# Output projection as seven block products with sums made under the gated merge, in a one-core encoder block

## The reference, cut to what matters

```
h  = rms_norm(x, norm_mix)                     # x: (1, 512, 1024) float32
q_a, k_a, v_a, q_b, k_b, v_b, u_c, g = split(h @ w_in)
o_a, o_b, o_c = attention_a, attention_b, pooling      # each (512, 512)
merged = sig(g0)*(o_a @ w_branch_a) + sig(g1)*(o_b @ w_branch_b) + sig(g2)*(o_c @ w_branch_c)
x  = x + merged @ w_out                        # (512, 1024) @ (1024, 1024)
h2 = rms_norm(x, norm_ffn)
x  = x + (silu(conv(gate)) * conv(val)) @ w_down,   [gate | val] = h2 @ w_up
```

## Time and profile before

| what | value |
|---|---|
| median of 3 executions | 823.93 us (823.73 to 824.07) |
| the profiled execution | 822.09 us, its span 820.2 us |
| granted TensorE clock, mean | 0.999 |
| TensorE busy | 813.5 us of the span (99%) |
| VectorE, ScalarE, GpSimd busy | 606.3, 407.4, 24.1 us |
| DMA traffic | 113.26 MB, mean 138 GB/s |

### The profile page before, as it was taken

How to read it: one execution, slowest core, us unless ns; L and a number is a source line. 1 busy time by engine, 2 the same in 40 slices (tenths; PEclk the granted TensorE clock), 3 DMA queues, 4 the chain that set the end, 5 groups by cost and what they waited for, 6 DMA issues and landing times.

```text
span 820.2 us, 11715 instructions
## 1 busy us (share of the span) xinstructions
PE 813.5 (99%) x3863; PEld 675.8 (82%) x3863; DVE 606.3 (74%) x893; ACT 407.4 (50%) x572; POOL 24.1 (3%) x42
## 2 busy tenths in 40 slices
PE   8999999999999999999999999999999999999998
PEld 6888888888888888888888888888888888888886
DVE  5958888868668775555554578777777878898797
ACT  6547676656545545434341464334433444565653
POOL 1010000000000060000000000000000000000000
PEclk9999999999999999999999999999999999999999
DMA  6342333222222223333367523665655555576454
GB/s 210 103 130 78 96 85 100 80 63 67 77 77 77 69 73 90 102 91 102 90 219 245 190 78 103 205 193 191 201 190 188 180 185 188 172 221 210 149 182 173
DMA packets 130702, 113.26 MB, mean 138 GB/s; under 512 B 6148, under 2 KB 109544, under 8 KB 129264
## 3 DMA queue, kind: packets, MB, share of 16 engines
q1 hardware_dynamic: 129840, 110.63, 43.0%
q0 software_dynamic: 672, 2.12, 0.9%
q10 hardware_dynamic: 160, 0.14, 0.0%
HBM read 99.21 MB, written 13.65 MB: 138 GB/s over the span
## 4 chain that ended last, share of the span: by engine, by line
PE 98%; DMA 1%; DVE 0%; SPq 0%; issue 0%; DVEq 0%
PE ps L1609 30%; PE ps L1610 30%; PE ps L1611 30%; PE ps L1741 2%; PE ps L1731 2%; PE ps L1756 1%; PE ps L1755 1%; DMA x_in<-in_x_dram 1%; PE ps L1909 0%; DVE out_sb L1594 0%; PE ps L1646 0%; PE ps L1705 0%; PE ps L1724 0%; PE ps L1706 0%; SPq L315 0%
## 5 line engine op out<-in xcount | busy, mean ns | idle before, releaser
L1609 PE MATMUL ps<-h_lo,w_hi 128*128 128x512 f32 x704 | 276.6, 393 | 0.1
L1611 PE MATMUL ps<-h_hi,w_lo 128*128 128x512 f32 x704 | 274.1, 389 | 0.0
L1610 PE MATMUL ps<-h_hi,w_hi 128*128 128x512 f32 x704 | 274.1, 389 | 0.0
L971 DVE TENSOR_TENSOR w_lo<-w_raw,w_hi 128x1024 fp32r<-128x1024 f32 x112 | 138.0, 1232 | 108.0 <-ACT w_hi L535 79.2
L535 ACT ACTIVATE w_hi<-w_raw 128x1024 fp32r<-128x1024 f32 x96 | 101.7, 1060 | 201.7 <-PE ps L1611 201.6
L1611 PEld LDWEIGHTS ps<-h_hi,w_lo 128*128 128x128 f32 x704 | 132.2, 188 | 27.9
L1609 PEld LDWEIGHTS ps<-h_lo,w_hi 128*128 128x128 f32 x704 | 132.2, 188 | 27.4 <-issue 0.3
L1610 PEld LDWEIGHTS ps<-h_hi,w_hi 128*128 128x128 f32 x704 | 132.3, 188 | 26.3
L1456 DVE TENSOR_TENSOR conv_in<-ps,r_ffn 128x512 f32<-128x512 f32 x44 | 30.3, 690 | 23.9 <-PE ps L1611 22.1
L890 ACT ACTIVATE conv_out<-conv_in,par 128x512 f32<-128x512 f32 x44 | 35.5, 806 | 9.7 <-DVE conv_in L1456 9.7
L1444 DVE SCALAR_TENSOR_TENSOR conv_out<-conv_in,par,conv_out 128x512 f32<-128x512 f32 x44 | 33.1, 752 | 5.0 <-DVE conv_out L1441 1.1
(11 more groups left out here) (238 smaller groups left out, 1304.1 us busy)
## 6 DMA issues: line engine op xcount, KB each, us to landing
w_raw<-in_w_in_dram SPq DMA_DIRECT2D x103, 256.0 KB, 3.1
w_raw<-in_w_up_dram SPq DMA_DIRECT2D x88, 256.0 KB, 3.2
raw_t<-in_w_down_dram SPq DMA_DIRECT2D x11, 1024.0 KB, 8.7
down_sums<-t_sum SPq DMA_DIRECT2D x11, 1024.0 KB, 5.7
w_raw<-in_w_down_dram SPq DMA_DIRECT2D x33, 256.0 KB, 3.0
w_raw<-down_sums SPq DMA_DIRECT2D x33, 256.0 KB, 3.9
w_raw<-in_w_out_dram SPq DMA_DIRECT2D x16, 256.0 KB, 3.2
w_raw<-down_sums SPq DMA_DIRECT2D x22, 128.0 KB, 3.0
```

What stands on the lines that cost most here:

```text
L971: v.tensor_tensor(w_lo[:, slot, :], w_raw[:, slot, :], r32(w_hi[:, slot, :]), ALU.subtract)\
L1609: mm3(dst, l_hi, r_lo, start=start, stop=False, **kw)
L1610: mm3(dst, l_hi, r_hi, start=False, stop=False, **kw)
L1611: return mm3(dst, l_lo, r_hi, start=False, stop=stop, **kw)
```

## The change

The output projection is written as a product of 2x2 blocks with seven products: the 1024 channels are four pairs p of two 128-channel blocks, the tokens two halves of 256, the columns two halves of 512.

- For each pair, `factor_sums` makes four sums of token halves of the merged blocks (`mst`), and `factors_hi`/`factors_lo` split seven 256-column factors (`mx_hi...`, `mx_lo...`). For pairs 0, 1 and 2 this stands inside the merge loop, for pair 3 behind it.
- For each pair, four sums of weight quarters are needed. GpSimd's queue loads the raw rows (1 MB), VectorE makes the sums (`set_of_sums`), GpSimd's queue stores them (1 MB). Six such sets (four of `w_out`, two of `w_down`) stand in the merge of blocks m = 1 to 6. The two of `w_down` were made in the output projection before.
- TensorE does pass X (four quarters of each pair, 96 matmuls) and pass Y (three quarters of each pair, 72 matmuls), adding Y onto banks that hold X's products. ScalarE keeps three products (`kept`), VectorE adds them into `x1`, which now holds the input from the start. The transposes behind it run in another order (`H2_ORDER`, `H2_BANK`).
- At the start, token tiles 1 and 2 are issued from ScalarE's queue, one dummy matmul more is done, and the transposes of tile 1 stand behind the first product, those of tiles 2 and 3 behind the second.
- The loops over m on ScalarE and VectorE are written out.

```
+NO = KD // 2
+MX = 7 * HT
+H2_ORDER = (4, 5, 6, 7, 0, 1, 2, 3)
+H2_BANK = (2, 3, 6, 7, 0, 1, 4, 5)
-WARM = (3, 3)
+WARM = (3, 4)
...
 SyncE
-            for t in range(1, TT):
-                x_load(t, 0)
+            x_load(3, 0)
...
+            def out_load(m, halves):
+                s, u = m // 2, m % 2
+                if m < 2:
+                    sp.wait_ge(lo_ready, N_OUT - 1 + u)
+                elif m == 3:
+                    sp.wait_ge(unit_done, N_OUT)
+                elif m > 3:
+                    sp.wait_ge(ow_lo, m - 3)
+                for dst, src in halves:
+                    sp.dma_start(dst, src).then_inc(d_landed[2 * (s % 2) + u], 16)
...
+            out_x(1, 0)
+            out_x(0, 0)
+            out_x(0, 1)
+            out_x(1, 1)
+            for p in (2, 3):
+                for u in range(2):
+                    out_x(p, u)
+            sp.dma_start(x1[:, :, :], xw).then_inc(x1_landed, 16)
+            out_y(0)
             pair_load(2)
+            for p in range(1, NO):
+                out_y(p)
...
 GpSimd
+            pool.wait_ge(pl_ready, 4)
+            for q in range(NO + 2):
...
+                pool.dma_start(wraw_o[:, :, :, :], rows_q).then_inc(set_landed, 16)
+                pool.wait_ge(t_ready, q + 1)
+                pool.dma_start(sums_q, wsum_o[:, :, :].rearrange("p (o j) c -> p o j c", o=1)).then_inc(set_stored, 16)
...
 ScalarE
+            for t in (1, 2):
+                a.dma_start(x_in[:, t, 0:WB], xw[:, t, 0:WB]).then_inc(x_landed[t][0], 16)
...
+            def factors_hi(p):
+                a.wait_ge(mst_ready, p + 1)
+                dst = factors(mx_hi01, mx_hi23, p)
+                act(dst[:, 0:HT], mp[:, 0, 0:HT], ACT.Copy)
+                act(dst[:, HT:5 * HT], mst[:, :], ACT.Copy)
+                act(dst[:, 5 * HT:MX], mp[:, 1, :], ACT.Copy).then_inc(mx_hi_ready, 1)
+
+            for m in range(KD):
+                i, n, last_m = m % 2, N_MERGE + 3 * m, m == KD - 1
+                ...
+                last.then_inc(sig_ab, 1)
+                hi(n + 2, i)
+                if last_m:
+                    out_hi(0)
+                else:
+                    hi(n + 3, 1 - i)
+                a.wait_ge(unit_done, n + 2)
+                if m:
+                    a.wait_ge(mg_ready, m)
+                act(mg[:, 3, :], ps[:, 4 * i + 2, :], ACT.Sigmoid, bias=pcol(BG, m + 2 * KD)).then_inc(sig_c, 1)
+                if last_m:
+                    out_hi(1)
+                else:
+                    hi(n + 4, i)
+                if m >= 2 and i == 0:
+                    factors_hi(m // 2 - 1)
...
+            for m in (2, 3, 4):
+                out_hi(m)
+            factors_hi(NO - 1)
+            for m in range(5, 10):
+                out_hi(m)
+            a.wait_ge(x1_acc, 1)
+            a.wait_ge(mx_lo_ready, NO)
+            kept(o1, 0)
+            a.wait_ge(ow_done, 2 * NO - 1)
+            kept(o5, 2)
+            out_hi(10)
+            a.wait_ge(ow_done, 2 * NO)
+            kept(o7, 6)
+            for m in range(11, 4 * NO):
+                out_hi(m)
...
+            a.wait_ge(ow_done, 4 * NO - 3)
             hi(N_UP, 0)
+            a.wait_ge(ow_done, 4 * NO - 2)
+            hi(N_UP + 1, 1)
             x1_square(0)
+            for j in range(4):
+                h2_split_hi(j)
             x1_square(1)
+            for j in range(4, KD):
+                h2_split_hi(j)
             x1_square(2)
             x1_square(3)
...
 VectorE
+            def set_of_sums(q):
+                d.wait_ge(set_landed, q * 16 + 16)
+                if q:
+                    d.wait_ge(set_stored, q * 16)
+                sums_first(wraw_o, wsum_o)
+                sums_second(q, wraw_o, wsum_o)
+
+            def factor_sums(p):
+                a11, a21, a12, a22 = mp[:, 0, 0:HT], mp[:, 0, HT:S], mp[:, 1, 0:HT], mp[:, 1, HT:S]
+                s2, s1, s3, s4 = (mst[:, q * HT:q * HT + HT] for q in range(4))
+                d.wait_ge(mg_ready, 2 * p + 2)
+                v.tensor_tensor(s1, a21, a22, ALU.add)
+                v.tensor_tensor(s3, a11, a21, ALU.subtract).then_inc(mst_step, 1)
+                ...
+                v.tensor_tensor(s2, s1, a11, ALU.subtract).then_inc(mst_step, 1)
+                ...
+                v.tensor_tensor(s4, a12, s2, ALU.subtract).then_inc(mst_ready, 1)
+
+            def factors_lo(p):
+                d.wait_ge(mx_hi_ready, p + 1)
+                dst, h = factors(mx_lo01, mx_lo23, p), factors(mx_hi01, mx_hi23, p)
+                v.tensor_tensor(dst[:, 0:HT], mp[:, 0, 0:HT], r32(h[:, 0:HT]), ALU.subtract)
+                v.tensor_tensor(dst[:, HT:5 * HT], mst[:, :], r32(h[:, HT:5 * HT]), ALU.subtract)
+                v.tensor_tensor(dst[:, 5 * HT:MX], mp[:, 1, :], r32(h[:, 5 * HT:MX]), ALU.subtract).then_inc(mx_lo_ready, 1)
+
+            for m in range(KD):
+                i, n, bank, last_m = m % 2, N_MERGE + 3 * m, 4 * (m % 2), m == KD - 1
                 lo(n + 2, i)
...
                 v.tensor_tensor(mg[:, 0, :], mg[:, 0, :], mg[:, 1, :], ALU.add).then_inc(mg_step, 1)
+                if last_m:
+                    out_lo(0)
+                else:
+                    lo(n + 3, 1 - i)
+                if m >= 2 and i == 0:
+                    factors_lo(m // 2 - 1)
                 d.wait_ge(sig_c, m + 1)
                 d.wait_ge(unit_done, n + 3)
                 v.tensor_tensor(mg[:, 2, :], ps[:, bank + 3, :], mg[:, 3, :], ALU.mult).then_inc(mg_step, 1)
                 d.wait_ge(mg_step, m * 3 + 3)
+                if m >= 2:
+                    d.wait_ge(mx_lo_ready, m // 2)
+                v.tensor_tensor(mp[:, i, :], mg[:, 0, :], mg[:, 2, :], ALU.add).then_inc(mg_ready, 1)
+                if last_m:
+                    out_lo(1)
+                else:
+                    lo(n + 4, i)
+                if i == 1 and not last_m:
+                    factor_sums(m // 2)
+                if 1 <= m <= NO + 2:
+                    set_of_sums(m - 1)
+
+            out_lo(2)
+            out_lo(3)
+            factor_sums(NO - 1)
+            out_lo(4)
+            factors_lo(NO - 1)
+            for m in range(5, 10):
+                out_lo(m)
...
+            out_lo(15)
             lo(N_UP, 0)
...
             lo(N_UP + 1, 1)
+            d.wait_ge(x1_acc, 3)
+            v.tensor_tensor(rows_of(0, 0), rows_of(0, 0), ps[:, 0:2, :], ALU.add).then_inc(x1_ready, 1)
+            d.wait_ge(ow_done, 4 * NO - 1)
+            d.wait_ge(x1_step, 5)
+            v.tensor_tensor(rows_of(0, 1), rows_of(0, 1), ps[:, 2:4, :], ALU.add).then_inc(x1_ready, 1)
+            for t in (2, 3):
...
+                v.tensor_tensor(x1[:, t, 0:S], x1[:, t, 0:S], ps[:, t + 4, :], ALU.add).then_inc(x1_ready, 1)
...
 TensorE
             x_transposes(0, 0)
             warm(1)
-            x_transposes(1, 0)
...
-                    if t == 0:
-                        x_transposes(kk + 2, 0)
+                    if t == 0 and kk == 0:
+                        x_transposes(1, 0)
+                    elif t == 0:
+                        x_transposes(2, 0)
+                        x_transposes(3, 0)
...
+            for p in range(NO):
+                start, stop, e = p == 0, p == NO - 1, p % 2
+                pe.wait_ge(mx_lo_ready, p + 1)
+                pe.wait_ge(ow_lo, 2 * p + 1)
+                first = out_quarter(p, 0, 0, e, 0, 0, start, stop)
+                ...
+                out_quarter(p, 2, 2, e, 0, 1, start, stop)[1].then_inc(ow_done, 1)
+                pe.wait_ge(ow_lo, 2 * p + 2)
+                if start:
+                    pe.wait_ge(mg_ready, KD)
+                sixth = out_quarter(p, 4, 1, e, 1, 0, start, stop)
+                ...
+                out_quarter(p, 6, 3, e, 1, 1, start, stop)[1].then_inc(ow_done, 1)
```

More of the change, by code:

```diff
@@ L51 @@
 N_OUT = N_MERGE + 3 * KD
-N_UP = N_OUT + KD
+N_UP = N_OUT
 N_DOWN = N_UP + 2 * KF
@@ L1884, in _ @@
                 merge(mm, 1, False)
-            def out_unit(k, slot, first=False, last=False):
-                pe.wait_ge(lo_ready, k + (N_OUT + 1))
-                pe.wait_ge(m_lo_ready, k + 1)
-                for b8 in range(8):
-                    t, h = b8 // 2, b8 % 2
-                    if first and b8 == 4:
-                        pe.wait_ge(mg_ready, KD)
-                    tk, c = slice(t * P, t * P + P), slice(h * S, h * S + S)
-                    done = product(ps[:, b8, :], m_hi[:, k, tk], m_lo[:, k, tk], w_hi[:, slot, c], w_lo[:, slot, c],
-                                   first, last)
-                    if last and (h == 1 or t == TT - 1) and b8 < 7:
-                        done.then_inc(x1_acc, 1)
-                done.then_inc(unit_done, 1)
@@ L1902, in _, with out_quarter @@
-            pe.wait_ge(mg_ready, KD - 1)
-            for k in range(KD):
-                out_unit(k, k % 2, first=k == 0, last=k == KD - 1)
+            def out_quarter(p, bank, at, e, u, h, start, stop, **kw):
```

(7 more changed lines are left out.)

285 lines of the change are left out of this document (166 added, 119 removed).

## The result

Six executions of the changed kernel take 852.66 us by their median (851.66 to 853.16), six of the kernel before 823.75 us (822.67 to 824.07). The ratio is 1.0355, with an interval of 1.0344 to 1.0365: 29 us slower, where I had forecast 3. The profiled execution's span is 851.5 us, 31.3 more than before.

A forecast was written before the change was run, and what follows sets the result against it. TensorE, busy 99% of the span, bounds the kernel. From the profiled 822.09 us: -5.4 matmuls, +7.3 factors, +1.0 output projection and transition, +0.1 start give 825.1, or 826.9 us as median (0.36% slower); range 823.4 to 831.5.

The forecast's parts named there:

- weight sums in the merge: Merge: VectorE's added sums fit and GpSimd's sets land in time; taken as 0, upper bound 4.4 us.
- Factors inside the merge: Merge blocks 2, 4, 6: factor work delays lo(n+4), stalling TensorE 2.45 us each; +7.3 us, bounds 6.6 to 8.1.
- Rival 5: Merge: clock drops to 1.2 GHz for 12 matmuls behind each stall; +8.2 us, 835.1 us in all; chance 0.05.
- Matmuls removed: Output projection: 168 matmuls instead of 192, at 0.227 us each; 5.4 us less.
- Output projection and transition: Output projection through transition to the up projection: thin places in operand supply cost 1.0 us, bounds 0.3 to 2.5.
- low part 4: Transition: this low part of the transposed operand comes after TensorE wants it; 0.65 us, up to 1.6.
- half-pair 10: Transition: its weights may land a microsecond late behind x1's 2 MB and `pair_load`'s 1 MB, raising 0.65 to 1.6 us.
- The stall for half-pair 5: Output projection: out_lo(5), behind the last pair's factor work, is ready at 13.8 but wanted at 13.6; 0.2 us.
- Start: Kernel start: second weight half may land later behind two token tiles; +0.1 us, bounds -0.2 to +1.3.
- Rival 4: Merge: sets come late because GpSimd's round trip takes 14 us; +4.4 on the forecast, 831.3 us; chance 0.10.

The follow-up runs named there:

- e4: Changed kernel with GpSimd's store and next set load held back until SP has issued the gate unit's weights: 836.31 us, ratio 1.0148.
- b2: Kernel before plus GpSimd's traffic alone (1 MB stored and 1 MB loaded in merge blocks 2 to 5, values unused): 829.07 us, ratio 1.0066.
- e2: Changed kernel with the sets' transfers cut to a sliver after the first set, so the right sums are left out: 835.43 us, ratio 1.0137.
- e3: Changed kernel with the factors' copies moved on ScalarE from behind hi(n+4) to behind hi(n+2): 834.98 us, ratio 1.0122.
- e5: Changed kernel with both merge mends, GpSimd's transfers held back and the factors' copies moved earlier: 828.16 us, ratio 1.0065.
- e8: Changed kernel with both merge mends, four output projection mends and the start of the kernel before: 820.96 us, ratio 0.9971.
- b1: Kernel before with the new start alone (token tiles from ScalarE's queue, one more dummy matmul, transposes reordered): 824.65 us, ratio 1.0014.
- e1: Changed kernel with the start of the kernel before: 851.8 us, ratio 1.0331.
- e7: Changed kernel with both merge mends, four output projection mends (x1 in pieces, `pair_load` later, two order changes) and the new start: 822.05 us, ratio 0.999.
- e9: Changed kernel with the four output projection mends alone, the merge as the change left it: 846.81 us, ratio 1.0295.
- e6: e5 with the x1 load in four pieces among the weight loads and the third down pair's load behind the last weights: 828.89 us, ratio 1.0064.

## Why the prediction was wrong

**The step that failed** is the one on the weight sums in the merge, "I take 0". I asked of GpSimd's 2 MB per block only whether the set itself lands in time for VectorE. It does: 7.9 us for the load, 4.8 for the store, and VectorE never stood for a set anywhere in the merge. I did not ask who is issued behind these transfers. Two engines are released by nearly the same moment, GpSimd by the last sum (352.5) and SP by the low part of unit n+2 that follows it (353.7), so the 2 MB stand in front of the one load with the least slack. The upper bound of 4.4 us was worked out from the wrong victim. What the runs showed in place of the 0: the waits in the merge are 19.0 us with the collision and 6.7 without it (e4), and the whole kernel takes 16.3 us less without it.

This step does not carry the whole miss. Without the collision e4 still takes 836.3 us, above my range, through the lower clock in the merge, the output projection and the start, which follow below.

**The two causes use up one slack.** The traffic alone costs 4.4 us of waiting in four blocks (b2), the order of the factors alone 6.7 in three (e4). Together they cost 19.0. In b2's expectation I called this multiplying; the working shows that the delays add in one chain, and the slack is taken off once. The gate unit has 5.4 us from the block's start until TensorE asks, and its own copy and subtraction take 2.4 of them. With the 0.2 at the block's start that leaves 2.8 us. In the border shown, the late load takes 3.2 (362.69 against 359.46) and the factors' work between the copy and its subtraction 5.2 (7.55 less 2.4): 3.2 + 5.2 - 2.8 = 5.6, and TensorE waited 5.33. Either alone would leave 0.4 or 2.4; e4 has 2.2 to 2.3, b2 0.7 to 1.5 (in the border shown its load came later still, 4.7 us into the block against 3.4). Taking away either one (e2, e4 the traffic, e3 the order) gave 16 to 18 us back, taking away both 24 (e5).

**Factors inside the merge: +7.3.** Right in place, sign and size: 2.18, 2.17 and 2.31 us in e4 against 2.45 each, 6.7 in all.

**Rival 5, the clock**, with 0.05 and +8.2 us. It was a rival to the forecast, and came with it: 8.1 us in the merge of the changed kernel, and about 1.6 in its output projection. That 8.1 meets the 8.2 is luck: the price was worked out for gaps of 2.4 us, and these are 6.3. At the size it was meant for, in e4, two of the three waits were followed by the lower clock, for 3.5 us in all. The chance of 0.05 was too low even there.

**Matmuls removed: -5.4.** The rate held (39.08 us busy for 168 matmuls in e8, 0.23 each), and 4.0 us of it were had there. In the changed kernel they were not.

**Output projection and transition: +1.0, bounds 0.3 to 2.5.** Mis-sized: 43.66 + 3.53 us less (38.1 + 3.8) is 5.3, and the wait for low part 4, which this term had in it too, lies behind that: 6.0 in all. I had put the 2 MB of x1 and the 1 MB of `pair_load` at a microsecond for half-pair 10; ScalarE stood 6.1 us for half-pair 8 and 2.5 for half-pair 10. TensorE waited 2.8 us in that stretch and lost 1.6 more to the lower clock. The low part 4 was rightly sized: 0.4 us of waiting, 0.7 with the restart, where I had 0.65. The stall for half-pair 5, put at 0.2, was 1.05 once the merge was mended (e5). This is the same mistake as in the merge, on SP's own queue.

**Start: +0.1, bounds -0.2 to +1.3.** About 1 us (b1 0.3 to 1.9; e1 and e8 0.9 and 1.1 less by medians than their twins with the new start). The weight half was late by the 1.5 us that I had kept as the worst case. The forecast did not have the clock's part in it: in the profiled execution the matmuls behind the late half ran at the lower clock.

**Two rules on transfers.** By the Trainium skill ("SBUF — State Buffer", section "Who interferes with whom"), what starves GpSimd of the port for its transfers' descriptors is VectorE in its two-port modes, and `tensor_tensor` has none. The trace agrees: VectorE's work in the merge is `tensor_tensor` but for two instructions, and with VectorE busy for 80.50 of 136.90 us the 1 MB loads landed after 7.6 to 9.1 us, where SP's took 8.7. Rival 4, the sets too late, did not come about. By the Trainium skill ("DMA: Bandwidth & Descriptors", section "Issuing engines are not separate DMA queues"), transfers of several issuers share the transfer engines. That is what the runs show in the merge: SP's load behind GpSimd's takes 8.1 us in place of 3.2. I had cited the rule for the start and not applied it to the merge, where it decided.

The 0.7 us in the later stages belong to the change: from the first product of the up projection to the end it is 349.1 us in the changed kernel and in e1 to e5, and 348.4 in the kernel before and in e7 to e9, where the wait for low part 4 does not show.

What stays open: why the output projection of e8 is still 1.4 us over 38.1, of which 0.5 is waiting, and why TensorE's clock rises early or late at the start.

## What to carry to other kernels

For every transfer that a change adds, list which transfers of other queues are issued in the microseconds behind it and what slack each has; that it lands in time for its own reader says nothing about them. Where two edits draw on the same slack, work out their joint delay, not the sum of two stalls. When a mend moves a large transfer, ask at once whose load now stands behind it: e6 gained nothing, e7, with the same transfer one place later and two changes of order besides, gained 7 us. And before reading a difference between two profiles, compare the clock at their starts.
